# Out-projections of the first two layers as three fp32r products

## What is computed

```python
o = jnp.concatenate([rms_norm(o_moba, g_moba_out), rms_norm(o_dsa, g_dsa_out)], axis=-1)
return o @ w_out              # (256 x 1024) @ (1024 x 1024)
# and behind it, in the block:
x = x + gt_m * rms_norm(y, g_post_mix[l])
h = rms_norm(x, g_pre_ffn[l]) * (1.0 + sc_f) + sh_f
```

## Time and profile before

| | us |
|---|---|
| median of 3 runs | 2484.81 (2483.03 to 2486.24) |
| profiled execution, its own time | 2486.55 |
| span in that execution | 2484.0 |
| layer 0, first and last out-projection matmuls start and end | 201.58, 230.15 |
| layer 1, the same | 591.94, 620.51 |
| layer 0, DVE's `summed(0)` ends, `gated(1, 1)` starts | 229.57, 230.18 |
| granted TensorE clock over the span, mean | 0.98 |

### The profile page before, as it was taken

The page is one execution under the profiler, slowest core; times in us unless marked ns, Lnnn a source line. Parts: engine busy times, 40 slices in busy tenths (PEclk is TensorE's granted clock), DMA queues, the critical chain, the costliest instruction groups (busy, mean ns, idle before and its releaser), DMA issues. The chain is left out here.

```text
span 2484.0 us, 38204 instructions
## 1 busy us (share of the span) xinstructions
PE 2376.0 (96%) x15277; PEld 1961.5 (79%) x15277; DVE 1721.4 (69%) x2003; ACT 1232.5 (50%) x1317; POOL 647.8 (26%) x347
## 2 busy tenths in 40 slices
PE   6999999899899998999988899999999999999997
PEld 4875999786799875899977478888888888888775
DVE  2565677474876775765587587878787878787576
ACT  2334543443544133333313376777767676767452
POOL 0000000000950261960063223232323232323113
PEclk9999999899999999999999899999999999999999
DMA  9897765457785585695533298999999999999672
GB/s 337 267 349 251 253 215 174 145 186 253 256 260 175 170 271 181 227 268 173 171 106 115 86 364 311 363 353 363 351 364 351 362 353 363 350 363 351 237 273 109
DMA packets 416671, 650.07 MB, mean 262 GB/s; under 512 B 37052, under 2 KB 255256, under 8 KB 416536
## 3 DMA queue, kind: packets, MB, share of 16 engines
q1 hardware_dynamic: 389328, 633.13, 73.6%
q10 hardware_dynamic: 27206, 15.03, 2.3%
HBM read 647.06 MB, written 1.05 MB: 261 GB/s over the span
## 5 line engine op out<-in xcount | busy, mean ns | idle before, releaser
L1602 ACT ACTIVATE region_part<-ring 128x2048 fp32r<-128x2048 f32 x412 | 770.0, 1908 | 272.7 <-PE bank L889 191.3
L2631 DVE TENSOR_TENSOR ring_part<-ring,region_part 128x2048 fp32r<-128x2048 f32 x240 | 569.8, 2403 | 48.9 <-PE bank L1223 23.0
L889 PE MATMUL bank<-ring_part,region_part 128*128 128x512 f32 x1480 | 578.8, 391 | 0.0
L887 PE MATMUL bank<-region_part 128*128 128x512 f32 x1288 | 512.2, 398 | 5.1 <-DVE region L2676 2.2
L888 PE MATMUL bank<-region_part 128*128 128x512 f32 x1152 | 449.4, 390 | 0.0
L1502 POOL TENSOR_TENSOR ring_part<-ring,region_part 128x2048 fp32r<-128x2048 f32 x48 | 248.2, 5178 | 509.7 <-ACT region_part L1602 423.1
L887 PE MATMUL bank<-xn_part,region_part 128*128 128x256 f32 x1152 | 326.8, 284 | 12.1 <-DVE hT_part L2232 10.2
L889 PEld LDWEIGHTS bank<-ring_part,region_part 128*128 128x128 f32 x1480 | 278.2, 188 | 60.1
L889 PE MATMUL bank<-hT_part,region_part 128*128 128x256 f32 x1152 | 324.7, 282 | 0.0
L888 PE MATMUL bank<-xn_part,ring_part 128*128 128x256 f32 x1152 | 324.5, 282 | 0.0
L2187 DVE TENSOR_TENSOR ring_part<-ring,region_part 128x2048 fp32r<-128x2048 f32 x72 | 175.7, 2449 | 177.7 <-ACT region_part L1602 177.7
(11 more groups left out here) (386 smaller groups left out, 3922.2 us busy)
## 6 DMA issues: line engine op xcount, KB each, us to landing
ring<-in_moe_w_gate SPq DMA_DIRECT2D x112, 1024.0 KB, 5.0
ring<-in_moe_w_up SPq DMA_DIRECT2D x112, 1024.0 KB, 5.1
ring<-in_moe_w_down SPq DMA_DIRECT2D x112, 1024.0 KB, 4.9
ring<-in_w_ada SPq DMA_DIRECT2D x48, 1024.0 KB, 9.5
ring<-in_mod_w SPq DMA_DIRECT2D x48, 1024.0 KB, 7.2
ring<-in_w_in SPq DMA_DIRECT2D x44, 1024.0 KB, 5.7
ring<-in_w_up_act SPq DMA_DIRECT2D x22, 1024.0 KB, 5.3
ring<-in_w_up_lin SPq DMA_DIRECT2D x22, 1024.0 KB, 5.6
```

Of the source, the lines that this page charges most:

```text
L887: nc.tensor.matmul(o, split(a_hi), split(b_hi), start=start, stop=False, skip_group_check=True)
L889: return nc.tensor.matmul(o, split(a_hi), split(b_lo), start=False, stop=stop, skip_group_check=True)
L1602: return nc.scalar.activation(out_, in_, func, **kw).then_inc(*done(*event))
L2631: v.tensor_tensor(split(w), w, whole(hi), ALU.subtract).then_inc(*done("moe_lo", j, e))
```

## The change

In layers 0 and 1 every out-projection matmul becomes a `product` of three fp32r matmuls. ACT writes the leading part of each `w_out` chunk (`out_leading`) into buffers that lie in dead parts of the attention's memory, and the leading part of the turned output into `oT_hi` in place of `hT`. DVE writes the low part of each chunk in place (`out_low`), and the low part of the turned output from the bank into `hT` (`o_low`). `oT_out` is now announced by DVE. On ACT, the leading part of the first up chunk waits for `("out", l, 1)` to be used up, since it is written where a buffer of `w_out` lies. Layers 2 and 3 keep their fp32 out-projections. `proj` is laid out 24 columns wider per token half, and what lies behind it moves.

```diff
+    rows_of = lambda at: region[:, at:at + SLOT].rearrange("p (k n) -> p k n", k=2)
+    out_hi = [rows_of(idx_at), rows_of(qk_at + 4 * S), proj[:, :, 0:D], proj[:, :, 1536:1536 + D]]
...
+    oT_hi = [(att_s.rearrange("p b s -> p (b s)") if k >= KD // 2 else ffn_rows)[:, k % (KD // 2) * S:(k % (KD // 2) + 1) * S] for k in range(KD)]
...
             def out_tokens(l, n, t):
 
                 key = ("out", l, n)
-                pe.wait_ge(*loaded(key))
+                pe.wait_ge(*(until("w_lo", *key) if l < 2 else loaded(key)))
...
-                        m = nc.tensor.matmul(y_tiles[2 * t + c], hT[:, kk, t * P:(t + 1) * P], w[:, k, c * 512:(c + 1) * 512],
-                                             start=kk == 0, stop=kk == KD - 1, skip_group_check=True)
+                        cs = slice(c * 512, (c + 1) * 512)
+                        if l < 2:
+                            m = product(y_tiles[2 * t + c], oT_hi[kk][:, ts], hT[:, kk, ts], out_hi[n][:, k, cs], w[:, k, cs], kk == 0, kk == KD - 1)
...
-                            run(hT[:, k, :], p_[:, i * S:(i + 1) * S], ACT.Copy, *name, scale=col(l, "g_moba_out", 1, k))
+                            run(split(oT_hi[k]), p_[:, i * S:(i + 1) * S], ACT.Copy, "act_chain", l, "oT", k, scale=col(l, "g_moba_out", 1, k))
+
+                def out_leading(n):
+                    act.wait_ge(*loaded(("out", l, n)))
+                    run(split(out_hi[n]), chunk(("out", l, n)), ACT.Copy, "w_hi", "out", l, n)
...
+                out_leading(0)
                 o_turned((0, 1))
+                out_leading(1)
                 o_squares(1, 1)
+                out_leading(2)
+                out_leading(3)
                 o_turned((2, 3))
...
+                if l < 2:
+                    act.wait_ge(*until("pe_used", "out", l, 1))
                 if l < 3:
                     leading(("up", l, 0, 0, 0))
...
+                def out_low(n):
+                    dve.wait_ge(*until("w_hi", "out", l, n))
+                    w = chunk(("out", l, n))
+                    v.tensor_tensor(split(w), w, whole(out_hi[n]), ALU.subtract).then_inc(*done("w_lo", "out", l, n))
+
+                def o_low(b):
+                    p_ = psum[bank_of["oT", l, b]]
+                    dve.wait_ge(*until("act_chain", l, "oT", 2 * b + 1))
+                    for i in range(2):
+                        k = 2 * b + i
+                        v.scalar_tensor_tensor(split(hT[:, k, :]), p_[:, i * S:(i + 1) * S], col(l, "g_moba_out", 1, k), whole(oT_hi[k]),
+                                               ALU.mult, ALU.subtract).then_inc(*(done("oT_out", l, b) if i else link()))
...
-                acc_out(l + 1, "mix", ADA_MIX - 1)
+                    if u == 12:
+                        out_low(0)
+                o_low(0)
+                o_low(1)
                 spread(1, 1)
                 finish(1, 1)
+                out_low(1)
+                acc_out(l + 1, "mix", ADA_MIX - 1)
+                out_low(2)
+                out_low(3)
+                o_low(2)
+                o_low(3)
```

11 lines of the change are left out of this document (8 added, 3 removed).

## The result

| | median, us | runs | range |
|---|---|---|---|
| kernel before | 2485.03 | 8 | 2483.03 to 2486.33 |
| changed kernel | 2493.09 | 8 | 2490.21 to 2495.11 |

The ratio is 1.0032, with a 95% interval from 1.0021 to 1.0043: 8 us slower, 5 to 11 by the interval. Both medians lie above the range on record, 2483.2 to 2491.2.

What follows compares the result with a forecast made beforehand. DVE's chain behind the out-projection's chunk 1, not PE, was taken to bound the stage; a start 3.4 us later outweighed cheaper matmuls, so two layers by 1.5 us added 3.0 us to 2484.81: 2487.8 us, range 2483.2 to 2491.2.

Steps and rivals of the forecast that it cites:

- Start: Layer 1's out-projection: PE starts at 595.35, 3.4 us later than before, behind four `o_low` of 0.45 us each.
- U: Moment at which chunk 1 of the out-projection is used up; forecast 608.85 against 606.64 before, 2.2 us later.
- Bank 5: First t = 1 product waits for the `mod_acc` copy until 599.3; PE held 1.2 us more, unless slower itself.
- Clock: Half clock behind PE's 3.2 us idle time before the out-projection loses 1.7 us, with 0 and 2.9 as ends.
- upper end of 2.9 us: Largest clock loss behind PE's idle time before the out-projection; part of a slower rival, 2489.2 to 2491.6 us, 24%.
- new wait: PE idle ahead of the first out-projection product, from 592.1 to 595.35, 3.2 us.
- rival without a fall: Clock doesn't fall behind PE's idle time before the out-projection: 1.0 us a layer later, 2486.8 us; 25%.
- U and behind: A 13.2 us chain puts DVE's t = 1 gating at 622.05; PE's last product ends at 619.75, 2.3 us ahead.
- The sum of the stages: Out-projection stages of layers 0 and 1 each 1.5 us later, 3.0 us together.
- The total: Two layers by 1.5 us make 3.0 us; against the median 2484.81 the forecast is 2487.8 us.
- No other stage changes.: All stages but the out-projections of layers 0 and 1 keep their time; shifted addresses costed at nothing.
- slower by over 0.2%: Whole kernel more than 5.0 us slower than before; given 18%.

Runs made afterwards that it cites:

- e5: Changed kernel with thirteen extra fp32 matmuls on PE in the wait before the first out-projection product of layers 0 and 1; 2491.2 us in one run.
- e7: Changed kernel with the first up chunk split behind t = 0's squares and sum in layers 0 and 1; 2485.55 us, ratio to before 0.9999.
- e12: Changed kernel with extra fp32 matmuls filling PE's two waits in layer 2; 2488.03 us, ratio to before 1.0009.
- e11: Kernel before with extra fp32 matmuls filling PE's two waits in layer 2; 2485.07 us, ratio to before 0.9994.
- e2: Changed kernel, unaltered, one run for a second profile; 2491.33 us.
- e1: Kernel before, unaltered, one run for a second profile; 2483.47 us.
- e8: Changed kernel with earlier `mod_acc` copy, earlier leading and low parts (chunk 0's low part on POOL), and the first up chunk's split later; 2476.95 us, ratio to before 0.9968.
- e9: Kernel before with scrap DVE products of 1024 and 690 columns ahead of t = 1's gating in layers 0 and 1; 2491.04 us, ratio 1.0020.
- e13: Changed kernel, unaltered, timed a second time on another chip; 2492.03 us, ratio to before 1.0024.
- e15: e8 with extra matmuls filling PE's two waits in layer 2; 2477.37 us, ratio to before 0.9963.

## Why the prediction was wrong

Right, by its steps, for layer 1; the times of the trace are lessened by the 0.2 us by which the layer began later:

- **Start.** `o_low` took 1.65 us for four, 0.41 each (0.45 taken, 0.40 to 0.63 as ends). PE starts at 595.1, forecast 595.35. The products took 0.231 us each, 48 of them in 11.09 us from U on (0.227 taken).
- **Bank 5.** The copy to `mod_acc` ended at 598.8, forecast 599.3. As forecast, the fall of the clock hid that wait; e5 showed it when the clock was kept up.
- **Clock.** Eight products at half clock, a loss of 1.7 us: 1.7 was taken. The upper end of 2.9 us was read from a row of 6 us that lies wholly inside a spell of 6.8 us; such a spell loses 3.4 us. Layer 1's new wait was followed by a spell in all seven traces that have it, layer 0's in four of seven. So the rival without a fall was true for layer 0 about half of the time.
- **U and behind.** SP issued the up chunk at 608.9, forecast 609.0; the chunk landed 5.3 us behind U; t = 1 was gated at 621.9, forecast 622.05, with no idle time. PE's last product ended at 619.8, forecast 619.75. e7 showed that the chain counts and not PE's end.
- **The sum of the stages.** 2 x 1.5 us forecast; 2.3 to 3.2 us in three traces, 3.4 us in e12's, and 2.96 us (2.0 to 4.5) in the time of e12 against e11. That the last agrees so closely is luck: single stages went from 0.9 us (layer 0, no spell behind the new wait) to 1.7 us.

The step that failed is one sentence under "The total": "No other stage changes." It was a term of zero, and it measured 3 to 5 us (6.1 and 8.1 between medians, less 3.0). What the runs showed in its place are half-clock spells behind two waits of layer 2 that had none before: 1.8 to 4.7 us in three traces, and gone in e12, where scrap matmuls fill these waits. In one of the three (e2) a longer spell at 469 us in layer 1 added as much again. The instructions of the other stages are the same and wait for the same things, which is what I had looked at. But their durations depend on the clock, and the clock on where their waits lie in time. The earlier trace rows had the warning in it: a wait of 2.9 us followed by a granted 0.52 in one place, one of 2.8 us by 0.72 in another, one of 2.1 us by 1.00 in a third. I read this as three prices of one new wait, to be weighed. It also allows that the third wait, at 947 us, costs something in another execution, and there are two such waits in layer 2 which cost nothing before. A bound from the same rows would have been 1.7 us for each, or 3.4 us (the first trace lost 4.7 us there, its second spell being 6.8 us long), which puts the upper end at 2494.6 (2491.2 + 3.4) instead of 2491.2, and the chance of "slower by over 0.2%" well over the 18% given.

The forecast also took one profiled execution as the kernel. A second one (e1) was 2.4 us shorter with the same instructions.

The section of the Trainium skill on HAM oscillation, in TensorE: Matmul & The Clock Gate, was cited for paying each time behind a wait. The page tells it of DMA waits of 3 to 5 us, while the new wait is 2.98 us and those of layer 2 are shorter. Layer 1's seven spells out of seven agree; layer 0's four of seven and layer 2's two waits (four and six of fourteen traces) do not. The same page of the Trainium skill bears on it more in Part 1, The HAM clock gate. It says that the gate's watch runs free of the program, so that the number of slow matmuls at a kernel's start varies between runs of one kernel, and it puts that cost below 1% of a typical span. The traces agree: the first spell of a trace, 35 to 40 us behind its start, lasts 6.8 us in four of seventeen (the changed kernel's first trace, e8, e9, e13) and 3.4 us in the others. They show such differences up to 950 us behind the start as well. 0.2% is 5 us here, and all that was to be forecast lay within that.

## What to carry to other kernels

A change that moves later work by a microsecond or two, in a kernel where PE has idle times of about 2 us ahead of dense matmuls, can turn these idle times into half-clock spells of 3.4 us or more; list them before the forecast and carry them into the range: in layer 2 a spell of 3.4 us cost 1.4 to 1.9 us, one of 6.8 us 3.1 us (e13). To learn what a change itself is worth, time it and its counterpart with these idle times filled by scrap matmuls: here that gave 2.96 us where the bare comparison gave 6.1 and 8.1.

When matmuls get cheaper, move what feeds the first one and what hangs on the last one in the same edit. The same 5.8 us a layer that made this kernel 8 us slower made it 9 us faster than before, once the low parts came earlier and the next chunk's split stood behind t = 0's normalisation. Beside a long subtraction on POOL look at every DVE instruction: here one went from 0.48 to 3.13 us.

## What the runs showed of the hardware

- A wait of 1.82 us of PE was followed by half clock in four of fourteen traces, one of 2.22 us in six of fourteen. Behind the wait of 1.82 us a spell made sixteen matmuls take 5.41 us and not 3.72.
- Spells of 3.4 us in layer 2 cost 1.4 to 1.9 us, one of 6.8 us 3.1 us. Behind the long spells of layer 3 nearly all traces lie alike against the clock (4.5 to 4.7 us from the wait at 1332 us to its spell in fifteen traces of sixteen).
- With scrap matmuls in the wait of 3 us (3.12 us of them) the products behind it ran at full clock at once, 0.23 us apart and not 0.43.
- While POOL subtracted 128x2048 (4.54 us), a DVE scaling of 128x512 that takes 0.48 us took 3.13 us, in four of four cases (both layers of e8 and e15). The copy out of a bank just before it kept its 0.69 us. Why is not shown; that the two share a port was a rival's guess.
